# Ten hand-laid places for the expert weights, loads begun behind mixer units, and an unrolled expert loop

## The reference, cut to what matters

```
h = x + Mixer(rms_norm(x))            # 3 gated branches from one input projection, merged, w_out
y = h + moe_ffn(rms_norm(h))          # then a final rms_norm
moe_ffn: top-1 of 4 groups, then top-2 of the 8 experts in it: 1088 token-expert pairs, 32 experts
  each expert: (silu(x @ w_gate[e]) * (x @ w_up[e])) @ w_down[e], scaled by the pair's gate
  w_gate[e], w_up[e]: 1024 x 512; w_down[e]: 512 x 1024, 2 MB each
```

## Time and profile before

| | |
|---|---|
| median of three runs | 1017.57 us |
| the profiled execution, whole | 1016.67 us |
| its span, first to last instruction | 1014.8 us |
| TensorE busy | 847.5 us (84%), 5203 matmul and 5203 weight-load records |
| VectorE / ScalarE / GpSimd busy | 353.5 / 201.0 / 79.9 us |
| moved by DMA | 261.93 MB, mean 258 GB/s |
| busiest stretch of the DMA engines | from 550 us to 940 us: 420 GB/s |

### The profile page before, as it was taken

How to read it: one execution, slowest core, us unless ns; L and a number is a source line. 1 busy time by engine, 2 the same in 40 slices (tenths; PEclk the granted TensorE clock), 3 DMA queues, 4 the chain that set the end, 5 groups by cost and what they waited for, 6 DMA issues and landing times.

```text
span 1014.8 us, 13052 instructions
## 1 busy us (share of the span) xinstructions
PE 847.5 (84%) x5203; PEld 579.0 (57%) x5203; DVE 353.5 (35%) x511; ACT 201.0 (20%) x300; POOL 79.9 (8%) x136
## 2 busy tenths in 40 slices
PE   3999999999999997995598887878788777787860
PEld 2999999999999997992233323222222222222220
DVE  3277686899567536216300000000000000000007
ACT  6321333222214323215001110000000000000003
POOL 0000000000000000000102111111111011110100
PEclk9999999999999998998699999999999999999995
DMA  9322221213311315439598999999999999999936
GB/s 305 82 84 84 83 84 54 84 43 116 113 63 64 104 43 203 147 154 358 208 401 338 421 420 420 420 419 419 421 419 421 419 421 421 419 421 420 419 130 260
DMA packets 73654, 261.93 MB, mean 258 GB/s; under 512 B 8999, under 2 KB 42947, under 8 KB 48480
## 3 DMA queue, kind: packets, MB, share of 16 engines
q1 hardware_dynamic: 68496, 252.44, 63.3%
q0 software_dynamic: 5120, 8.93, 2.4%
HBM read 256.08 MB, written 13.74 MB: 266 GB/s over the span
## 4 chain that ended last, share of the span: by engine, by line
PE 63%; DMA 27%; DVE 5%; issue 2%; ACT 2%; SPq 1%; DVEq 0%; POOLq 0%; POOL 0%; ACTq 0%
PE ps L654 30%; DMA gu<-in_w_up_e 25%; PE ps L897 15%; PE ps L689 9%; PE ps L918 4%; PE ps L622 1%; PE ps L783 1%; PE ps L886 1%; SPq L540 1%; DVE xh L1617 1%; DVE xh L1624 1%; PE ps L908 0%; DVE xh L1616 0%; PE ps L849 0%; PE ps L836 0%
## 5 line engine op out<-in xcount | busy, mean ns | idle before, releaser
L1580 DVE TENSOR_TENSOR work<-ps,ffn_cols 128x512 f32<-128x512 f32 x32 | 22.1, 692 | 442.3 <-PE ps L886 442.3
L654 PE MATMUL ps<-x_high,w_high 128*128 128x272 f32 x640 | 174.1, 290 | 0.0
L654 PE MATMUL ps<-x_low,w_high 128*128 128x272 f32 x640 | 173.3, 290 | 0.0
L897 PE MATMUL ps<-gu,work 128*64 128x512 f32 x512 | 118.6, 617 | 18.4 <-DMA gu<-in_w_up_e 15.8
L654 PE MATMUL ps<-x_high,w_low 128*128 128x272 f32 x640 | 132.9, 289 | 0.0
L897 PE MATMUL ps<-slot,work 128*64 128x512 f32 x480 | 111.3, 618 | 22.6 <-issue 21.8
L654 PEld LDWEIGHTS ps<-x_low,w_high 128*128 128x128 f32 x640 | 121.1, 189 | 0.1
L654 PEld LDWEIGHTS ps<-x_high,w_high 128*128 128x128 f32 x640 | 121.0, 189 | 0.1
L654 PEld LDWEIGHTS ps<-x_high,w_low 128*128 128x128 f32 x640 | 100.5, 189 | 0.0
L897 PEld LDWEIGHTS ps<-gu,work 128*64 128x64 f32 x512 | 38.1, 142 | 97.9 <-issue 96.5
L897 PEld LDWEIGHTS ps<-slot,work 128*64 128x64 f32 x480 | 40.0, 141 | 92.8 <-issue 91.8
(11 more groups left out here) (238 smaller groups left out, 950.7 us busy)
## 6 DMA issues: line engine op xcount, KB each, us to landing
ring<-in_w_down_e SPq DMA_DIRECT2D x16, 2048.0 KB, 22.5
gu<-in_w_gate_e SPq DMA_DIRECT2D x16, 2048.0 KB, 17.1
gu<-in_w_up_e SPq DMA_DIRECT2D x16, 2048.0 KB, 23.4
slot<-in_w_gate_e SPq DMA_DIRECT2D x15, 2048.0 KB, 17.1
slot<-in_w_up_e SPq DMA_DIRECT2D x15, 2048.0 KB, 23.4
slot<-in_w_down_e SPq DMA_DIRECT2D x15, 2048.0 KB, 21.8
w_raw<-in_w_in SPq DMA_DIRECT2D x22, 1024.0 KB, 5.1
w_raw<-in_w_out SPq DMA_DIRECT2D x4, 1024.0 KB, 4.9
```

The lines of the kernel that those rows point to most:

```text
L654: last = pe.matmul(ps[:, 2 * r + half, 0:HT], w[:, k, c * P:(c + 1) * P], part[:, k, half * HT:(half + 1) * HT], start=(k == 0 and len(par ...
L897: last = pe.matmul(ps[g * CAP:(g + 1) * CAP, 2 + s].rearrange("p (m f) -> p m f", m=2), xgT[s][:, k % 4, (k // 4) * CAP:(k // 4 + 1) * CAP ...
L1580: v.tensor_tensor(xgT[s].rearrange("p c (h m) -> p c h m", h=2), ps[:, s].rearrange("p (c h m) -> p c h m", c=4, h=2), wide(ffn_cols[:].re ...
```

## The change

- All weight places and mixer buffers become parts of one tensor `mem`, laid out by hand. In it are ten places of 2 MB (16 KB a partition) for expert weights, `PLACES`. Transfer number n = 3 e + (0 gate, 1 up, 2 down) goes to place n mod 10, so any transfer may reuse the place of the one ten before it.
- The first five transfers are issued behind mixer units: gate 0 and up 0 behind the first two units ("branch", 2, ·), down 0 and gate 1 behind ("out", 0) and ("out", 1), up 1 behind ("out", 3). Down 1, gate 2 and up 2 follow as w_out ends, down 2 after the stored rows have landed (before: issued ahead of that wait), gate 3 after the first two gathers.
- From then on each of the 86 transfers left waits for the one that frees its place (`gu_done` or `dn_done`).
- `final_row` is loaded after the last expert weights are issued, not after expert 2.
- All five engines' expert loops are written out in full: no hardware loop over experts is left. GpSimd indexes `block_rows` directly, and the copies into `idx_now` are gone, except for further blocks.
- TensorE's order with AHEAD = 0 is `gate_up(0)`, `turn_rows(1)`, `turn_hidden(0)`, `down(0)`, and then the order of the old loop from expert 1 on.
- Each matmul of `gate_up` reads its two matrices as a pair of columns some distance apart (`pair_columns`), the lower place first, so `silu` and `times_up` take the half in which the gate or the up product lies.

```diff
+    PLACES = [0, UNIT, X, X + UNIT, X + 2 * UNIT, WEIGHTS + 2 * UNIT, WEIGHTS, WEIGHTS + UNIT, M_HIGH + UNIT, M_HIGH]
+    def place_of(e, what):
+        return number(e, what) % NP
...
+    AHEAD = 0
...
+        def load_part(e, what, place):
+            sp.dma_start(part(PLACES[place], UNIT).rearrange("p (h n) -> p h n", h=2), expert_part(e, what)).then_inc(unit_loaded[place], 16)
+
+        PRELOADED_BEHIND = {
+            ("branch", 2, 0): [(0, GATE, ("branch", NJ - 1, 3))],
+            ("branch", 2, 1): [(0, UP, ("branch", NJ - 1, 3))],
+            ("out", 0): [(0, DOWN, ("gate2", 1, 3))],
+            ("out", 1): [(1, GATE, ("gate2", 1, 3))],
+            ("out", 3): [(1, UP, ("branch2", 1, 3))],
+        }
...
             sp.wait_ge(*unit_used(n - 3))
             load_unit(n)
+            if units[n] in PRELOADED_BEHIND:
+                for e, what, used in PRELOADED_BEHIND[units[n]]:
+                    sp.wait_ge(product, made[used])
+                    load_part(e, what, place_of(e, what))
...
-        load_gate_up(1, 1, 0)
         sp.wait_ge(product, N_B + NCH)
-        load_down(0, 0)
+        load_part(1, DOWN, place_of(1, DOWN))
         sp.wait_ge(half_rows, 3)
-        load_gate_up(0, 0, 0)
+        load_part(2, GATE, place_of(2, GATE))
         sp.wait_ge(product, N_O)
-        load_gate_up(0, 0, 1)
-        load_gate_up(1, 1, 1)
-        load_down(1, 1)
+        load_part(2, UP, place_of(2, UP))
...
-        load_down(2, 2)
         sp.wait_ge(xn2_stored, 16 * NCH)
+        load_part(2, DOWN, place_of(2, DOWN))
         for c in range(2):
             sp.wait_ge(xg_loaded[c], 16)
-        for m in range(2):
-            load_gate_up(2, 2, m)
...
+        load_part(3, GATE, place_of(3, GATE))
+        for e in range(3, NE):
+            for what in (GATE, UP, DOWN):
+                n = number(e, what) - NP
+                if n >= 0:
+                    sp.wait_ge(dn_done if n % 3 == DOWN else gu_done, n // 3 + 1)
+                    load_part(e, what, place_of(e, what))
+        sp.wait_ge(dn_done, NE - 3)
         sp.dma_start(final_row, d["final_norm_g"].partition_broadcast(P)).then_inc(norm_rows_loaded, 16)
-        with sp.Fori(0, NE // 2 - 3) as i:
-            for s in range(2):
-                load_expert(2 * i + 5 + s, s, 2 * i + 4 + s)
-        load_expert(NE - 1, 0, NE - 2)
...
+        turn_rows_of(0)
+        gate_up_of(0)
+        turn_rows_of(1)
+        for e in range(AHEAD):
+            gate_up_of(e + 1)
+            finish(e)
+            turn_rows_of(e + 2)
+        finish(AHEAD)
+        for e in range(AHEAD + 1, NE):
+            gate_up_of(e)
+            if e + 1 < NE:
+                turn_rows_of(e + 1)
+            finish(e)
...
-            g.tensor_copy(idx_now[:, s:s + 1], block_rows[:, bass.ds(e, 1)]).then_inc(gather_idx[s], 1)
-            pool.wait_ge(gather_idx[s], turn + 1)
-            pool.sem_inc(waits_met, 1)
             pool.indirect_dma_start(xg[s], None, xn2_dram.rearrange("t (h n) -> (t h) n", h=2),
-                                    bass.IndirectOffsetOnAxis(ap=idx_now[:, s:s + 1], axis=0),
+                                    bass.IndirectOffsetOnAxis(ap=rows, axis=0),
```

More of the change, by code:

```diff
@@ L162, in program @@
[L162 to L171, removed]
@@ L181, in program, with part, rows_of @@
[L181 to L185, removed]
+    def part(first, n):
+        return mem[:, first:first + n]
+    def rows_of(first, q, n):
+        return part(first, q * n).rearrange("p (q t) -> p q t", t=n)
@@ L186, in program @@
+    mid = part(MID, 4736)
     x = xh[:].rearrange("p (c n) -> p c n", n=D)
@@ L223, in program @@
[L223 to L229, removed]
+    yb, yc = rows_of(YL + KW * T, KW, T), rows_of(YC, KW, T)
@@ new lines, in program, with take, scratch @@
+    sgu_rows = part(YL + KW * T, 2 * W).rearrange("p (a n) -> p a n", n=W)
+    wsT = rows_of(YL + KW * T + (KW - 1) * T, KW, P)
+    states = part(YL, 4 * W).rearrange("p (a n) -> p a n", n=W)
+    SPARE = [(M_HIGH + 2 * UNIT, X), (X + 3 * UNIT, WEIGHTS), (LATE, MEM)]
+    at = [first for first, _ in SPARE]
+    def take(area, n):
+        first = at[area]
+        at[area] += n
+        assert at[area] <= SPARE[area][1]
+        return first
+    def scratch(area, *shape):
+        v = part(take(area, int(np.prod(shape))), int(np.prod(shape)))
+        return v.rearrange("p (a b) -> p a b", b=shape[1]) if len(shape) == 2 else v
@@ new lines, in program, with number @@
+    yo = [scratch(2, W) for s in range(2)]
+    xg = [scratch(2, W) for s in range(2)]
+    hT = [scratch(2, 2, P) for s in range(2)]
+    xgT = [scratch(0, 4, P) for s in range(2)]
+    sig = [scratch(1, 256) for s in range(2)]
+    hid = [scratch(1, 256), scratch(2, 256)]
+    at = [first for first, _ in SPARE]
+    PLACES = [0, UNIT, X, X + UNIT, X + 2 * UNIT, WEIGHTS + 2 * UNIT, WEIGHTS, WEIGHTS + UNIT, M_HIGH + UNIT, M_HIGH]
+    GATE, UP, DOWN = range(3)
+    NP = len(PLACES)
+    def number(e, what):
+        return 3 * e + what
@@ new lines, in place_of, with loads_of, unit, pair_columns @@
+    def place_of(e, what):
+        return number(e, what) % NP
+    def loads_of(e, what):
+        return number(e, what) // NP + 1
+    spare_places = [n % NP for n in range(3 * NE - NP, 3 * NE)]
+    def unit(place, lines):
+        return part(PLACES[place], UNIT).rearrange("p (k n) -> p k n", k=lines)
+    def pair_columns(places, k, first):
+        low, high = sorted(PLACES[place] for place in places)
+        columns = mem[:, low + k * DE + first:][:, 0:256]
+        return bass.AP(columns.tensor, columns.offset, [columns.ap[0], (high - low, 2), (1, 256)])
@@ L231, in program, with gate_up_places, gate_half, up_half @@
+    def gate_up_places(e):
+        return place_of(e, GATE), place_of(e, UP)
+    def gate_half(places):
+        return slice(0, 256) if PLACES[places[0]] < PLACES[places[1]] else slice(256, 512)
+    def up_half(places):
+        return slice(256, 512) if PLACES[places[0]] < PLACES[places[1]] else slice(0, 256)
+    final_row = part(PLACES[spare_places[0]], D)
+    over_places = spare_places[3:6]
     const = {k: cst[:, v] for k, v in CONST.items()}
@@ L887, in turn_rows, with gate_up @@
             last.then_inc(xg_turned, 1)
-        def gate_up(e, s, w, loads, free):
+        def gate_up(e, s, places, loads, free):
             pe.wait_ge(xgT_ready, e + 1)
-            pe.wait_ge(gu_loaded[w], loads * 32)
+            for what in (GATE, UP):
+                pe.wait_ge(unit_loaded[places[what]], loads[what] * 16)
             if free is not None:
```

315 lines of the change are left out of this document (144 added, 171 removed).

## The result

The changed kernel takes 1006.61 us (median of 1007.17, 1006.05, 1004.31 us and one disturbed run of 1478.58 us, which the ratio leaves out) against 1017.24 us for the kernel before: ratio 0.9887, 95% interval 0.9867 to 0.9908, a gain of 10.6 us between these medians and of 11.5 us by the ratio (9.4 to 13.5 by its interval), where 7.2 were forecast. The time lies in the range given.

What follows compares the result with a forecast made beforehand. The 16 DMA engines were taken as the bound from about 558 us. Places -15.0, copy -0.3 and code +8.1 gave -7.2 us: 1009.5 us profiled, 1010.4 us as median, range 1001.5 to 1016.5 us.

Steps and rivals of the forecast that it cites:

- Bound and arithmetic: Expert loads: time is the moment the DMA engines stay full, plus experts left at 15.79 us each, plus a fixed tail.
- Ten places, -15.0 us: Expert weight loads: DMA engines full from 506.03 us, 86 transfers of 5.26 us left, ending at 958.7 against 973.7 us.
- rival A: Written-out expert loops: code costs nothing, packets spread or on an engine with room; 1002.3 us, chance 0.23.
- The copy, -0.3 us: GpSimd before the first gather: dropping the index copy saves 0.3 us, bounds 0.2 to 1.2 us.
- Written-out loops, +8.1 us: Expert loops: 12.3 TensorE code packets of 1.08 us on one DMA engine, 13.3 us less 5.2 us of standing.
- the lone engine at 437 us: End of a 2 MB load: one DMA engine busy 1.1 us longer, read as code falling on one engine.
- The serial order, 0: TensorE, experts 0 to 2: not running gate_up(e + 1) ahead of down(e) costs 0, at 13.27 us per expert under 15.79.
- B: Written-out loops: the code's DMA engine already lands last, so nothing is absorbed; slower, 1019.9 us, chance 0.12.
- C: Mixer's w_out: early loads delay its first units' casts, up to 4.6 us on the sum, 1015.0 us, chance 0.08.
- D: Start of the full stretch: the gap is not filled, start later than 506 us; 1012 to 1017 us, chance 0.05.

Runs made afterwards that it cites:

- a_halves: Changed kernel with up 3, down 3, up 4 and down 4 loaded in halves, first halves as soon as their places' halves are read; 1001.37 us.
- a_np9: Changed kernel with nine places instead of ten, gate 3 loaded by the loop and final_row one down later; ratio 0.9922 to the kernel before.
- a_late_wout: Changed kernel with the early loads of down 0 and gate 1 behind w_out's units 2 and 3, not 0 and 1; ratio 0.9861 to the kernel before.
- b_unroll_pe: Kernel before with only TensorE's expert loop written out; ratio 0.9992 to the kernel before.
- b_code_more: Kernel before with TensorE's expert loop written out and 90 already met waits more per expert on TensorE from expert 9; ratio 0.9995 to the kernel before.
- a_pad_pool3: Changed kernel with 260 already met waits more on GpSimd behind each of the first 30 scatters; ratio 1.0027 to the kernel before.
- a_ahead2: Changed kernel with AHEAD = 2, the order of before for experts 0 to 2; ratio 0.9903 to the kernel before.
- a_shallow20: Changed kernel where SyncE waits, from expert 20 on, for the use six parts back instead of ten; ratio 0.9867 to the kernel before.

## Why the prediction was right and wrong

**Bound and arithmetic.** Right: the time is the moment from which the DMA engines stay full, plus the parts left at 5.26 us, plus the tail. a_halves moved the moment and a_np9 the number of parts, and the end followed both.

**Ten places, -15.0 us.** The mechanism is right and the size somewhat high. In a_late_wout, which had no low clock at the start, the releases came at 505.95, 512.35 and 519.22 us as I had them. From the first release the sum has (971.64 - 15.3) - (506.03 - 0.3) = 450.6 us to the last gate_up without any code; that execution took 958.52 - 505.95 = 452.6 us. Of the 2.0 us between, 1.1 are a term that I left out: a fuller stretch also holds more of the experts' own gathers and scatters. The changed kernel had 4720 of their packets for 85 parts where before's rate would give 85 x 4240 / 80 = 4505; 215 packets are 2.7 transfers of 80, at 0.41 us. The mean share of the code, 0.23 MB at 419 GB/s, is 0.5 us. The last 0.4 us is open.

**The profiled execution.** It had 1.9 us more at the start (507.61 us against 505.7) and the dip of 1.0 us, both beside a clock below full, and 0.8 us in the tail, where the other executions have 43.0 to 43.5 us as before had. -15.0 - 0.3 + 1.9 + 1.0 + 2.0 + 0.8 = -9.6, against -9.4 in the spans. These last four are the 5.7 us that the sum did not have; without them, and without its 8.1 us for code, it would have been rival A's time.

**The copy, -0.3 us.** The gather before starts at 491.93 us, after at 492.48, but relative to the routing products ahead of it 0.32 us sooner; it agrees in size, and no run tried it alone.

**Written-out loops, +8.1 us.** This step failed. Count (14 against 12.3) and size of the packets were right. What failed is the inference from one row, a share of 0.05 for 1.1 us, that the packets always meet the same engine and that it has average standing. b_unroll_pe and b_code_more put it at 0 with 12 and 15 packets, and the lone engine at 437 us stays unexplained. I had noted that the engine was seen lagging once and not twice, and gave rival A only 0.23. The Trainium skill, "Runtime: NRT & Kernel Launch", section Instruction fetch mechanics, calls the crossing of a block mostly hidden: for TensorE's code the runs agree, with 0 us for 12 packets; a_pad_pool3, with 14 us for 30 more packets of GpSimd's code, shows where it doesn't hold.

**The serial order, 0.** Wrong in its reason. I compared TensorE's pace with the DMA engines', as if only the average counted. At the start the order decides when the second place comes free: by a_ahead2's trace it gains 3 us. The sum was not hurt, since its releases at 512 and 519 us silently took the serial order for granted.

**Rivals.** A was right on the code, and its 1002.3 us is missed by the 2.0 us above and the executions' clock. B fell with b_unroll_pe, C with the w_out stages. D holds in small, 1.9 us of later start in the profiled execution.

## What to carry to other kernels

Where the DMA engines are the bound, count from the moment at which they stay full: draw up which use frees which place at what time over the first few tiles, since the order of two products there is worth more than the same order later, and everything else that moves bytes in the stretch is paid in full. Free a place in halves if the reader reads it in halves. Don't price code loading by one lagging engine: write out one loop alone and time it; it was free for one engine's code here and cost about its whole time for another's.

## What the runs showed of the hardware

- Instruction packets of TensorE (q8, 16 KB, 1.08 us of one engine) cost nothing beside full weight loads, 12 to 15 of them (b_unroll_pe, b_code_more); those of GpSimd (q14, 8 KB) cost 14 us when 30 more of them came, and left one DMA engine 8 us and more behind the other 15. The Trainium skill, "DMA: Bandwidth & Descriptors", section Queues, rings and completion order, lets each DMA engine take turns between queues; no run here shows why the one queue's packets gather on an engine and the other's don't.
- SyncE's issue takes 0.4 us, but 5 to 11 us once about 34 us of 2 MB transfers (six to seven) are outstanding. It is then on the chain of waits, with 10% of the span, and yet costs nothing: with fewer outstanding (a_shallow20) the pace was 174.5 us for 11 experts, with the full queue 174.6.
- One stage of 35 us took about 1 us longer in half of the 14 traces (granted clock 0.85 against 0.90), with the change and without it. A difference of 1 us between two single traces proves nothing before it has been seen in a kernel without the change.
